# Attention in a float32 kernel: the product with the values in plain float32, one step later

## The reference, cut to what matters

```python
def diff_attend(q, k, v, lam):
    s = jnp.einsum('bqhcd,bkhcd->bhcqk', q, k) * (DIFF_QK_DIM ** -0.5)
    p = jax.nn.softmax(s, axis=-1)
    pd = p[:, :, 0] - lam * p[:, :, 1]
    return jnp.einsum('bhqk,bkhd->bqhd', pd, v)

y = concat([conv_mixer(p[..., :COL_CONV], conv_w),
            sub_ln(o, subln_g, lam_init)]) @ w_out_mix
h = post_norm_residual(h, y, g1, ln_g, ln_b)
```

## Time and profile before

| what | value |
|---|---|
| runs | 3317.8, 3315.67, 3316.4 us |
| span of the profiled execution | 3312.7 us (no time of its own is given beside it) |
| TensorE busy | 3142.2 us (95%) |
| VectorE busy | 2118.3 us (64%) |
| ScalarE busy | 1329.6 us (40%) |
| GpSimd busy | 960.4 us (29%) |
| mean granted clock | 0.983 |

### The profile page before, as it was taken

The page is one execution under the profiler, slowest core; times in us unless marked ns, Lnnn a source line. Parts: engine busy times, 40 slices in busy tenths (PEclk is TensorE's granted clock), DMA queues, the critical chain, the costliest instruction groups (busy, mean ns, idle before and its releaser), DMA issues.

```text
span 3312.7 us, 36526 instructions
## 1 busy us (share of the span) xinstructions
PE 3142.2 (95%) x14623; PEld 2589.1 (78%) x14623; DVE 2118.3 (64%) x2816; ACT 1329.6 (40%) x1877; POOL 960.4 (29%) x425
## 2 busy tenths in 40 slices
PE   7999888889999999978899999998999899999997
PEld 3888777778888888767788888887887788888886
DVE  4725477676777777585766565567697655555554
ACT  4311588454333333442633333335227443333332
POOL 0001466244444443310443333313000022222220
PEclk9999999999999999989999999999999999999999
DMA  7435211212233322111011111111111111111121
GB/s 231 145 115 178 88 45 49 89 44 72 101 102 102 102 98 81 45 41 51 26 57 52 51 51 51 51 58 52 32 52 58 58 45 51 51 51 51 51 64 51
DMA packets 190482, 235.72 MB, mean 71 GB/s; under 512 B 9671, under 2 KB 149562, under 8 KB 190314
## 3 DMA queue, kind: packets, MB, share of 16 engines
q1 hardware_dynamic: 173338, 172.90, 16.8%
q10 hardware_dynamic: 8352, 30.41, 2.6%
q0 software_dynamic: 8624, 30.09, 2.4%
HBM read 217.64 MB, written 15.73 MB: 70 GB/s over the span
## 4 chain that ended last, share of the span: by engine, by line
PE 74%; DVE 13%; ACT 8%; issue 3%; DMA 1%; POOL 0%; DVEq 0%; SPq 0%; ACTq 0%; POOLq 0%
PE psum L609 24%; PE psum L610 24%; PE psum L611 24%; DVE page_r L620 2%; DVE small L1413 2%; DVE small L742 1%; DVE PT_lo L620 1%; ACT temp L923 1%; ACT page_r L615 1%; ACT prob L1379 1%; DVE U_lo L620 1%; ACT U_hi L615 1%; DMA page<-in_ada_w_dram 1%; DVE H L1525 1%; PE psum L788 1%
## 5 line engine op out<-in xcount | busy, mean ns | idle before, releaser
L609 PE MATMUL psum<-U_hi,page_r 128*128 128x512 f32 x2108 | 832.4, 395 | 23.9 <-DVE page_r L620 11.1
L610 PE MATMUL psum<-U_lo,page_r 128*128 128x512 f32 x2108 | 826.2, 392 | 0.0
L611 PE MATMUL psum<-U_hi,page_r 128*128 128x512 f32 x2108 | 826.0, 392 | 0.0
L620 DVE TENSOR_TENSOR page_r<-page,page_r 128x1024 fp32r<-128x1024 f32 (+2 forms) x239 | 344.4, 1447 | 357.8 <-ACT page_r L615 350.6
L615 ACT CAST page_r<-page 128x1024 fp32r<-128x1024 f32 (+2 forms) x323 | 337.4, 1047 | 397.6 <-DVE page L640 95.2
L609 PEld LDWEIGHTS psum<-U_hi,page_r 128*128 128x128 f32 x2108 | 399.3, 189 | 117.3 <-DVE page_r L620 16.2
L611 PEld LDWEIGHTS psum<-U_hi,page_r 128*128 128x128 f32 x2108 | 399.0, 189 | 84.2
L610 PEld LDWEIGHTS psum<-U_lo,page_r 128*128 128x128 f32 x2108 | 399.4, 189 | 81.1
L609 PE MATMUL psum<-page_r,act_page_r 128*128 128x512 f32 x1176 | 457.5, 389 | 0.0
L610 PE MATMUL psum<-page_r,act_page_r 128*128 128x512 f32 x1176 | 457.5, 389 | 0.0
L2243 ACT ACTIVATE temp<-psum 128x512 f32<-128x512 f32 x192 | 114.6, 597 | 849.9 <-PE psum L611 805.6
(11 more groups left out here) (343 smaller groups left out, 4594.7 us busy)
## 6 DMA issues: line engine op xcount, KB each, us to landing
page<-in_mlp_w_dram SPq DMA_DIRECT2D x128, 512.0 KB, 4.1
page<-in_ada_w_dram SPq DMA_DIRECT2D x48, 512.0 KB, 5.0
page<-in_w_in_dram SPq DMA_DIRECT2D x38, 512.0 KB, 4.1
page<-in_w_up_dram SPq DMA_DIRECT2D x32, 512.0 KB, 4.1
page<-in_w_down_dram SPq DMA_DIRECT2D x32, 512.0 KB, 4.1
ada_land<-in_ada_w_dram ACTq DMA_DIRECT2D x24, 512.0 KB, 4.4
sum_page<-in_ada_w_dram ACTq DMA_DIRECT2D x12, 512.0 KB, 5.5
act_page<-in_ada_w_dram ACTq DMA_DIRECT2D x12, 512.0 KB, 8.6
```

The source lines that it names most:

```text
L609: pe.matmul(out, l_hi, r_hi, start=start, stop=False, skip_group_check=read_between)
L610: pe.matmul(out, l_hi, r_lo, start=False, stop=False, skip_group_check=read_between)
L611: return pe.matmul(out, l_lo, r_hi, start=False, stop=stop, skip_group_check=read_between)
L620: return dve.tensor_tensor(lo, src, hi.bitcast(F32), ALU.subtract).then_inc(*k.lo.inc(*key))
```

## The change

The product with the values is made from the transposed weights and the values as they are, in float32: ten matmuls of 128 columns instead of twenty of 256 in float32r. Weights and values are no longer split. The values of a head are loaded straight into their own tile (`V`, two of 5 KB a partition), and the transposed weights have two buffers. The product moves one step later in TensorE's order, and the output and its sum of squares by two iterations. VectorE's coefficient moves to the next iteration, behind the first maximum. ScalarE's weighting of component 1 moves from the head of its iteration to behind the first exponential and the third cast. ScalarE now makes the sum of squares, for each step. GpSimd makes the low parts of output weights 0 to 4. The first two convolution tiles are done in TensorE's iterations 32 and 33, in banks 0, 1 and 3, 4.

```diff
+        self.PT = [place(f"PT{i}", h_at + (4 + i) * row, [P, KEYS // P, P]) for i in range(2)]
+        self.V = [place(f"V{i}", split_at + (10 + 25 * i) * KB, [P, KEYS]) for i in range(2)]
...
+            if u.att and u.att[0] == "v":
+                u.raw, u.left_by = self.V[u.att[1] % 2], self.values_left(u)
+                continue
...
+    def values_left(self, u):
+        h = u.att[1]
+        return [("done", self.att["v", h - 2, 0].s if h >= 2 else self.first["conv"] + 10 + h)]
...
+def pe_weigh_values(k, pe, on, i):
+    h, qt = STEPS[i]
+    if qt == 0:
+        for key in (("x", h, 0), ("v", h, 0)):
+            on.wait_ge(*k.landed(k.att[key]))
+    k.banks.take(on, ("O", i), (k.dve_done, ("O", i)), slot=O_BANK)
+    out = k.psum[:, O_BANK, 0:P]
+    for j in range(KEYS // P):
+        on.wait_ge(*k.hi.at("PT", i, j // 4))
+        m = pe.matmul(out, k.PT[i % 2][:, j, :], k.V[h % 2][:, j * P:(j + 1) * P], start=j == 0, stop=j == KEYS // P - 1)
+    m.then_inc(*k.pe_done.inc("O", i))
...
 def pe_attention(k, pe, on):
-    for i in range(len(STEPS) + 2):
+    for i in range(len(STEPS) + 3):
...
+        if i >= 3:
+            pe_weigh_values(k, pe, on, i - 3)
+        if i in CONV_TILE_AT:
+            tt, first = CONV_TILE_AT[i]
+            pe_conv_tile(k, pe, on, tt, (first, first + 1))
+    k.banks.n = 6
...
-WEIGHTS_AT_STEP = {26: (0,), 28: (1,), 32: (2,), 33: (3, 4)}
+WEIGHTS_AT_STEP = {27: (0,), 28: (1,), 32: (2, 3), 34: (4,)}
+CONV_TILE_AT = {32: (0, 0), 33: (1, 3)}
...
-def dve_gated_weights(k, dve, on, s):
+def pool_gated_weights(k, pool, on, s):
     u = k.split[s]
     k.wait_left(on, u.before)
-    dve_lo(k, dve, on, u.lo, u.raw, u.hi, "w", s)
+    on.wait_ge(*k.hi.at("w", s))
+    pool.tensor_tensor(u.lo, u.raw, u.hi.bitcast(F32), ALU.subtract).then_inc(*k.pool_lo.inc("w", s))
...
 act_attention
+    for i in range(len(STEPS) + 4):
+        if 0 <= i - 2 < len(STEPS):
+            turned(i - 2, 0)
+            turned(i - 2, 1)
+        if i < len(STEPS):
+            exponential(i, 0)
+        if 0 <= i - 2 < len(STEPS):
+            turned(i - 2, 2)
         if 0 <= i - 1 < len(STEPS):
             p1 = k.prob1[(i - 1) % 2]
             on.wait_ge(*k.scaled.at("coefficient", i - 1))
             act.activation(p1[:], p1[:], ACT.Copy, ...)
...
         if i < len(STEPS):
             exponential(i, 1)
...
+        if i >= 4:
+            h, qt = STEPS[i - 4]
+            on.wait_ge(*k.dve_done.at("O", i - 4))
+            on.wait_ge(*k.act_done.now())
+            act.activation(k.temp[3][:, 0:P], k.O[qt // TPC][:, qt % TPC, h * P:(h + 1) * P], ACT.Square,
+                           accum_out=k.sumsq[:, qt, h:h + 1]).then_inc(*k.act_done.inc("sumsq", i - 4))
...
 dve_attention
+    for i in range(len(STEPS) + 4):
+        if i >= 4:
+            ...output of step i - 4 from PSUM, times 1 / sum
+        if i < len(STEPS):
+            maximum(0, i)
+        if 0 <= i - 1 < len(STEPS):
+            ...reciprocal and coefficient of step i - 1
+        if i < len(STEPS):
             maximum(1, i)
...
 pool_attention
+        if i == len(STEPS) + 3:
             ...reload of H, behind the product of the last step
+        for n in WEIGHTS_AT_STEP.get(i, ()):
+            pool_gated_weights(k, pool, on, k.first["mix"] + n)
```

More of the change, by code:

```diff
@@ L325, in allocate @@
         self.ada_in = [d(f"ada_in{i}") for i in range(4)]
+        self.v_in = [d(f"v_in{i}") for i in range(2)]
         self.h_dma = [d(f"h_dma{i}") for i in range(TT)]
@@ L508, in place_units @@
             u.left_by = left[u.page]
+            if u.att and u.att[0] == "x":
+                u.left_by = u.left_by + self.values_left(u)
             left[u.page] = [("taken", u)]
@@ L514, in place_units @@
                 what, h, i = u.att
+                if what == "v":
+                    continue
                 if what == "q":
@@ L517, in place_units @@
                 elif h >= 2:
-                    last = [self.att["k" if what == "k" else "v", h - 2, i].s]
+                    last = [self.att["k", h - 2, j].s for j in ((i,) if what == "k" else (0, 1))]
                 elif h == 1:
@@ L569, in landed, with landing, low_done @@
             return self.ada_in[u.n % (2 * FB) % 4].at(u.n)
-        return self.raw_in[u.page].at(u.n)
+        return self.landing(u).at(u.n)
+    def landing(self, u):
+        return self.v_in[u.att[1] % 2] if u.att and u.att[0] == "v" else self.raw_in[u.page]
+    def low_done(self, s):
+        return (self.pool_lo if self.first["mix"] <= s < self.first["mix"] + GATED else self.lo).at("w", s)
     def wait_left(self, on, ends):
@@ L600, in sync_program @@
         for dst, src in u.pieces:
-            sp.dma_start(dst(u.raw), src).then_inc(*k.raw_in[u.page].inc())
-        k.raw_in[u.page].also(u.n)
+            sp.dma_start(dst(u.raw), src).then_inc(*k.landing(u).inc())
+        k.landing(u).also(u.n)
     for t in range(TT):
@@ L1246, in low_att_unit @@
         last = engine.tensor_tensor(KK[low, i, 0:T], u.raw[low, :], KK[low, i, 0:T].bitcast(F32), ALU.subtract)
[L1247 to L1252, removed]
-    else:
-        last = engine.tensor_tensor(V[:, 1, 0:T], u.raw[:], V[:, 0, 0:T].bitcast(F32), ALU.subtract)
+    else:
+        last = engine.tensor_tensor(KK[low, :, T:KEYS], u.raw[low, 0:2 * CTX].rearrange("p (c n) -> p c n", c=2),
+                                    KK[low, :, T:KEYS].bitcast(F32), ALU.subtract)
     last.then_inc(*k.att_lo.inc("w", u.s))
@@ L1276, in pe_turn_weights @@
     p0 = k.prob0[i % 3]
-    k.banks.take(on, ("PT", i, part), (k.lo, ("PT", i, part)), slot=b)
+    k.banks.take(on, ("PT", i, part), (k.hi, ("PT", i, part)), slot=b)
     for j in range(n):
@@ L1414, in maximum @@
             *k.measured.inc("max", c, i))
[L1416 to L1423, removed]
-            maximum(0, i)
[L1425 to L1428, removed]
-            maximum(1, i)
[L1430 to L1453, removed]
-            dve.tensor_tensor(sq[:], o, o, ALU.mult).then_inc(*k.step.inc())
-            on.wait_ge(*k.step.now())
-            dve.tensor_reduce(k.sumsq[:, qt, :], sq[:].rearrange("p (h d) -> p h d", h=HEADS), AX_X, ALU.add).then_inc(
-                *k.dve_done.inc("sumsq", qt))
@@ L1461, in dve_attention @@
                    "conv", c, j)
-    for n in WEIGHTS_AT_STEP[len(STEPS) + 1]:
-        dve_gated_weights(k, dve, on, k.first["mix"] + n)
 def pool_attention(k, pool, on):
@@ L1471, in pool_attention @@
     pool.dma_start(k.conv_in[:], k.d_conv.rearrange("k p t -> p k t")).then_inc(*k.conv_read.inc())
-    for i in range(len(STEPS) + 1):
-        if i:
+    for i in range(len(STEPS) + 4):
+        if 0 <= i - 1 < len(STEPS):
             p0, p1 = k.prob0[(i - 1) % 3], k.prob1[(i - 1) % 2]
             on.wait_ge(*k.att_lo.now())
+            on.wait_ge(*k.pool_gated.now())
+            on.wait_ge(*k.pool_lo.now())
             on.wait_ge(*k.act_done.at("p1", i - 1))
@@ L1498, in a_operands, with pe_down_tile @@
     return k.A_hi[:, j, s], k.A_lo[:, j, s]
-def pe_down_tile(k, pe, on, stage, tt, units, operands, ready):
-    banks = [k.banks.take(on, ("down", stage, tt, half), (k.h_added, (stage, tt, half))) for half in range(2)]
+def pe_down_tile(k, pe, on, stage, tt, units, operands, ready, slots=(None, None)):
+    banks = [k.banks.take(on, ("down", stage, tt, half), (k.h_added, (stage, tt, half)), slot=slots[half]) for half in range(2)]
     for j, u in enumerate(units):
-        on.wait_ge(*k.lo.at("w", u.s))
+        on.wait_ge(*k.low_done(u.s))
         ready(j, tt)
@@ L1528, in dve_down_tile, with pe_conv_tile @@
         m.then_inc(*k.h_added.inc(stage, tt, half))
+def pe_conv_tile(k, pe, on, tt, slots=(None, None)):
+    pe_down_tile(k, pe, on, "mix0", tt, [k.unit("mix", j) for j in range(FB)], lambda j, tt: u_operands(k, 0, j, tt),
+                 lambda j, tt: on.wait_ge(*k.lo.at("u", "conv", 1, 3)), slots)
 def pe_mix_out(k, pe, on):
```

92 lines of the change are left out of this document (37 added, 55 removed).

## The result

The changed kernel takes 3354.6 us (median of 4 runs, 3348.2 to 3358.2) against 3317.1 before: a ratio of 1.0104, 95% interval 1.0090 to 1.0118. It is slower, as forecast, but by 37.5 us where the sum said 21.9, and 2.6 us above the forecast's range.

A forecast was written before the change was run, and what follows sets the result against it. A loop of waits paces attention; most of the kernel is TensorE matmuls left untouched. 8.9 + 0.2 + 6.8 + 4 + 2 = 21.9 us, added to the span 3312.7 and 3.7 around it, gives 3338 us, range 3321 to 3352.

The forecast's parts named there:

- the loop: Attention step: weighting, mix, transposes, casts, exponential and weighting again form one round of 7.57 us; +8.9 us by the 32nd weighting.
- The rival on the faster side: Attention steps: mixing is not in the round, ScalarE sets a pace of mean 6.1 us; 3287 us, chance 0.10.
- The product: TensorE's product with the values: ten float32 matmuls take 2.13 us per step; TensorE's step of 5.5 us is not the bound.
- The transfers moved past queues: Value transfers, a step later, cost nothing; mixing-weight loads come some 10 us later; H's reload, at 8.6 us, is just under cover.
- first weighting after that: Start of attention: the first weighting waits for the first exponential and starts 3.2 us later, at 378.76.
- 31 steps: round, gate step, clock: Attention steps: rounds of 7.57 us against 7.35 before, +0.2 for step 27's gate work on GpSimd, +4 for the clock.
- end of the stage, clock included: From the 32nd weighting to the third convolution tile: +6.8 us, plus 2 for the clock after two long gaps.
- The 3.7 us that the prediction put around the span: Whole kernel: the runs' median, 3316.4 us, exceeds the trace's span, 3312.7, by 3.7, added again to the forecast span.
- The clock: TensorE idles 2.1 us per attention step, sometimes dropping to 1.2 GHz; 0.80 us more per hit on eight transposes, 4 us taken.
- each hit shrinks the next gap: Attention steps: the reason given for taking 4 us of clock loss where the hits alone would cost 6 to 8.
- my own bracket: Attention steps: a quarter to a third of the steps hit by the low clock, costing 6 to 8 us.
- units of other heads "fit": Attention steps: a cast on ScalarE and 2.39 us on GpSimd for other heads fit within the 7.57 us round.

The follow-up runs named there:

- The two experiments on the weighting's place: Weighting back at head of its iteration, VectorE's coefficient first, in changed kernel: 3296.0 us; old kernel with weighting behind first exponential and third cast: 3341.3 us.
- The filled gap: Changed kernel plus six unused float32 identity products on TensorE ahead of each step's first transposes, from the third step on: 3345.2 us, ratio 1.0084.
- The experiment on the tiles: Changed kernel with the two moved convolution tiles back behind the last product: 3343.1 us, ratio 1.0074.
- the last kernel: Changed kernel with weighting and coefficient first, convolution tiles behind the last product, and VectorE's low part one iteration later: 3291.8 us, ratio 0.9921.

## Why the prediction was right, and what was mis-sized

**What bounds, and the loop: right.** The round named from one step of the old trace is the chain of the new one, link for link, at 7.7 to 7.8 us; the transposes' idle time is released by the mix. The two experiments on the weighting's place show it as cause. The rival on the faster side (mixing not in the round) fell for this order and came true with the other, a little below what it promised: 6.47 us a step and 3296 us, where it said 6.1 and 3287.

**The product: right.** Twenty records in 2.40 us, the next scores 2.15 us after the first (2.13 predicted); ScalarE's squares with their accumulator reads 0.4 us (607.50 to 607.93; 0.36 predicted), no table load among them; neither is in the round. The transfers moved past queues cost nothing: no wait of TensorE in the stage ends with one, and H's first addition starts at 667.06, as the last normalization ends.

**The sum**, at the third tile (669.42 against 629.23, +40.2), by the prediction's terms:

| term | predicted | measured |
|---|---|---|
| start of the stage (first scores 371.07, before 366.92) | 0 | +4.2 |
| first weighting after that | +3.2 | +2.5 |
| 31 steps: round, gate step, clock | 5.7 + 0.2 + 4 = 9.9 | 253.4 - 227.8 = 25.6 |
| end of the stage, clock included | 6.8 + 2 = 8.8 | 33.8 - 25.8 = 8.0 |

I do not count the first row as an effect of the change: first scores stand at 366.4, 367.1 and 368.3 in three executions of the changed kernel edited only behind that point, and at 366.9 in the kernel before. By the medians the difference is 37.5; the two profiled spans differ by 43.7, the changed kernel's being its slowest run. The 3.7 us that the prediction put around the span were too many: where a run's own time and span are known, they differ by 2.4 us before and 1.8 in the change.

**The step that failed is the size of the 31 steps**, 15.7 us short, in three parts. The clock: I took 4 us, arguing that "each hit shrinks the next gap". Ten steps hold transposes at 1.2 GHz and are 0.7 to 1.6 us longer than their neighbours, 9.9 us together; an eleventh, with its scores alone at that level (546.20), is 0.4 longer. The argument held for one step only: the gap behind eight of the ten is 1.20 to 1.40 us, but ScalarE and GpSimd were delayed with TensorE, and two steps later it is back at 1.8 to 2.0. The number of hits lay in my own bracket (a quarter to a third); the price of one was too low, since the chain of a slow step runs on from the transposes through the second scores to the last transposes (529.79 to 533.66), where a plain round leaves TensorE after four transposes. The filled gap takes 8.2 us out of the steps. The round: 7.72 instead of 7.57, 4.5 us over 30 steps. I let the second copy follow the eighth transpose (1.04 + 0.04 + 0.47 = 1.55); from transposes' start to copies' end the chain shows 1.83, since the first copy waits for the four transposes of its bank and the second follows it; the other links were 0.13 shorter in all. The steps 4 to 11: 8.2 instead of 7.7, 4 us. I said that units of other heads "fit" and gave the convolution's no term; that VectorE's low part would be stretched and hold up the output and the first maximum I did not see. These three, the eleventh slow step and a last step 0.8 longer make 9.9 - 4 + 4.5 + 4 + 0.4 + 0.8 = 15.6.

**The end: right**, by mechanism and in its sum: gaps of 1.33 and 0.69 us inside tile 0 released by GpSimd (2.2 and 1.1 predicted, each more than half too long), 6.54 us idle ahead of the head transposes (6 predicted). The experiment on the tiles gives back 8.9 us by the third tile (y+24.9 in place of y+33.8) and 10 by the ratio.

## What to carry to other kernels

When a step of a software pipeline moves within an engine's queue, write down the round that it closes (whose output it waits for, who waits for its own) and add its links up: the busy shares fell here and the time rose. An instruction on the round goes first in its iteration, work that hides a later chain stays beside that chain, and an idle gap of TensorE near 2 us in each step is priced with the steps at half clock that it can bring (here ten of 31), the chain behind them included.

## What the runs showed of the hardware

VectorE and GpSimd hold each other up in these traces where both read two operands from on-chip memory (SBUF). VectorE's low part (128x512) takes 0.69 us and 1.7 beside GpSimd's mix. In the change, an operation on 128x1 stands thus beside GpSimd:

```profile
420.79 2.63 POOL L1259 TENSOR_TENSOR Q_lo<-page,Q_hi 128x1024 fp32r<-128x1024 f32 x1
422.96 0.47 DVE L1453 SCALAR_TENSOR_TENSOR small<-small,lam 128x1 f32<-128x1 f32 x1
```

Both end at 423.4; alone it takes 0.22 us. In all such rows that I read, the VectorE operation ends with GpSimd's, or a working time of 0.6 us after it; reductions that read the scores' banks keep their 1.48 us, and the reciprocal, with one operand, its 0.15 to 0.17 (393.77 to 393.94, inside the mix at 392.50). GpSimd loses less: its mix took 3.25 and 3.40 us beside the low part in the last kernel, 2.9 elsewhere. No idle time shows it, only the duration. By the Trainium skill (SBUF — State Buffer, "Who interferes with whom") the two share one pair of ports, an exclusive lock that the instruction issued first holds to its end, against a VectorE instruction with two operands in that memory and not, outside its two-port modes, against one with a single such operand. The rows agree in both halves (in the pair at 492.67 and 492.69 the starts are too close to tell the order), and show what the forecast left out: the price is the rest of a whole GpSimd instruction, 2.2 us where 0.22 grew to 2.40, however small the blocked one is.

The length of TensorE's gap alone does not say whether the clock falls. In the change it fell after gaps of 1.84 us (488.97 and 513.15), of 1.90 (529.79), of 1.92 to 2.00 and, in the scores only, of 1.89 (546.20), and stayed at 1.00 over the four microseconds behind five gaps of 1.89 to 1.91 (at 412.52, 562.00, 585.18, 592.95 and 600.72). In the change with the low part later it stayed at 1.00 after one of 2.09 (472.66). Behind gaps of 1.20 to 1.40, which follow slow steps, it stayed at 1.00 each time. What decides between them these runs leave open.
